# Another order of the 24 convolution units in the preparation of a gated delta rule: q before k in each head

## The chip, the core and the metric

The kernel runs on one core of one Trainium2 chip, written directly for its engines: TensorE (PE), VectorE (DVE), ScalarE (ACT), GpSimd (POOL) and the DMA queues, which run side by side and wait for each other on semaphores. The metric is the time of one execution on the device in microseconds; lower is better. All data is float32.

## The reference

The program is a network of two blocks on a sequence of 512 tokens of width 1024. The first block has differential attention, a gated delta rule in both directions and an expert-choice feed-forward layer of 16 experts; the second has a sparse attention mixer and a gated recurrence. The change lies in the preparation of q, k and v for the gated delta rule:

```python
h = rmsnorm(x, norm1_w[l])
p = jnp.einsum('bsd,dn->bsn', h, w_in[l])
...
qkv_g = jax.nn.silu(centred_depthwise_conv(qkv_g, conv_w[l]))   # 5 taps, each channel by itself
qg, kg, vg = jnp.split(qkv_g, [GDN_QK, 2 * GDN_QK], axis=-1)    # 8 heads of 128 each
qg = l2norm(qg.reshape(b, s, GDN_HEADS, GDN_DK))
kg = l2norm(kg.reshape(b, s, GDN_HEADS, GDN_DK))
vg = vg.reshape(b, s, GDN_HEADS, GDN_DV).astype(jnp.float32)
g_f = -jnp.exp(a_log_fwd[l]) * jax.nn.softplus(a_f + dt_bias_fwd[l])
...
o_fwd = gated_delta_rule_chunked(qg, kg, vg, g_f, beta_f)
```

## The kernel before

The kernel is a row of stages, each a block in which every engine has its own list of instructions; a stage ends when all its engines have ended. The stages are: norm and transposes, projections of the attention's q, k, v with rotation, attention (in whose gaps the first eight channel groups of the delta rule's input are already projected), the preparation that the change touches, the delta rule, output projections, the experts, and the second block.

In the preparation the 3072 channels are 24 units of 128 channels by 512 positions: unit h is q of head h (0 to 7), 8 + h is k, 16 + h is v. The eight q units lie ready in X (`raw_of`, units below `NEAR`). The k and v units have still to be projected by PE, each by eight matmuls (`project`, line 625), into one of four PSUM banks. The list `SEQ` gives the order in which units are worked on; before, it is k, q, v of head 0, then k, q, v of head 1, and so on. For one unit the work is:

- DVE: the convolution over five taps, one scaling (line 732) and four multiply-adds (line 735), into one of three buffers `conv[p % 3]`.
- ACT: silu in place (line 696). For q and k also the square (line 701) into one of two buffers `sq`.
- q and k: PE sums the square over the 128 channels with a matmul by ones (`sums`, line 634); ACT makes of it the reciprocal root by a logarithm and an exponential (`norm`, lines 199 and 200), behind a load of the function table (line 677; silu needs a load of its own, line 694); DVE multiplies (line 750), which ends the unit.
- k and v: PE turns the unit by four transposes (`turn`, line 649) and ACT copies the result out (`evac_turned`, line 685).

Every engine works strictly through its own list, and the lists are written out by hand. PE for head i: project v(i), sum k(i), project k(i+1), sum q(i), turn k(i), turn v(i). DVE: the convolutions in the order of `SEQ`, and behind the convolution at place p the multiplication of the unit at place p - 2. ACT: silu and square of k, silu and square of q, norm of k, silu of v, norm of q, the two evacuations. Beside this the gates of all heads are prepared once: small operations on DVE at its places 0 and 1, three small matmuls (lines 660 and 662) and three small exponentials (lines 710 to 712).

Of the kernel before, what the change touches and what calls it, by code (L numbers as in the profile page):

```python
# [14 lines left out]
ALU = mybir.AluOpType  # L15
ACT = mybir.ActivationFunctionType
# [7 lines left out]
HEADS = 8  # L24
# [87 lines left out]
def build(nc, io):  # L112
    ctx = ExitStack()
    counts = {}
    with ctx:
# [5 lines left out]
        def sem(name):  # L121

            return cleared.pop(0) if cleared else ctx.enter_context(nc.semaphore(name))
# [63 lines left out]
        def A():  # L187
            return Chain(nc.scalar, act_link, counts)
# [26 lines left out]
        def slab(slot, k=KD, cols=512):  # L215
            return SLB[slot][:, 0:k * cols].rearrange("p (k n) -> p k n", k=k)
# [198 lines left out]
        with nc.Block() as block:  # L415
# [177 lines left out]
        conv = [R[6][:, i * S:(i + 1) * S] for i in range(3)]  # L593
        sq = [R[6][:, 1536 + i * S:2048 + i * S] for i in range(2)]
        p3_done, conv_done, silu_done, sq3, ss3, rstd3, qk_norm, tr3, tr3_evac = [
            sem(n) for n in ("p3_done", "conv_done", "silu_done", "sq3", "ss3", "rstd3", "qk_norm", "tr3", "tr3_evac")]
        pre = {n: sem("p_" + n) for n in ("u_ready", "sp_ready", "g_ready", "cum_done", "G_ready", "pre_ready")}
        NC3 = 3 * HEADS

        SEQ = [u for i in range(HEADS) for u in (HEADS + i, i, 2 * HEADS + i)]  # L600
        POS = {u: p for p, u in enumerate(SEQ)}
        FAR = [u for u in SEQ if u >= NEAR]
        AT = {u: n for n, u in enumerate(FAR)}
        NORMED = [u for u in SEQ if u < 2 * HEADS]
        NTH = {u: n for n, u in enumerate(NORMED)}
# [8 lines left out]
        with nc.Block() as block:  # L614
            @block.tensor
            def _(pe):

                def project(n):
                    u = FAR[n]
                    i, j = (u - NEAR) // 4, u % 4  # L620
                    pe.wait_ge(slab_in[i], 48)
                    if n >= 4:
                        pe.wait_ge(conv_done, POS[FAR[n - 4]] + 1)
                    for k in range(KD):
                        m = pe.matmul(PS[n % 4][:, :], slab(i)[:, k, j * P:(j + 1) * P], hT[:, k, :],  # L625
                                      start=(k == 0), stop=(k == KD - 1))
                    m.then_inc(p3_done, 1)

                def sums(u):
                    n = NTH[u]  # L630
                    pe.wait_ge(sq3, n + 1)
                    if n >= 2:
                        pe.wait_ge(rstd3, n - 1)
                    pe.matmul(PS[4 + n % 2][:, :], ones, sq[n % 2], start=True, stop=True).then_inc(ss3, 1)

                def turn(u):
                    n = AT[u]
                    if u in NTH:
                        pe.wait_ge(qk_norm, NTH[u] + 1)
                        src = gk[:, u - HEADS, :]  # L640
                    else:
                        pe.wait_ge(silu_done, POS[u] + 1)
                        src = conv[POS[u] % 3]
                    if n >= 2:
                        pe.wait_ge(tr3_evac, n - 1)
                    else:
                        pe.wait_ge(pre["sp_ready"], 2)
                    for t in range(NT):
                        m = pe.transpose(PS[6 + n % 2][:, t * P:(t + 1) * P], src[:, t * P:(t + 1) * P], ident)
                    m.then_inc(tr3, 1)  # L650

                project(0)
                for i in range(HEADS):
                    k, q, v = SEQ[3 * i:3 * i + 3]
                    project(2 * i + 1)
                    sums(k)
                    if i == 0:
                        pe.wait_ge(pre["g_ready"], 1)
                        for d in range(2):
                            pe.matmul(v16(PS[6][:, 0:64])[:, :, 8 * d:8 * d + 8], (tri_le, tri_ge)[d],  # L660
                                      v16(gg)[:, :, 8 * d:8 * d + 8], start=True, stop=True)
                        pe.matmul(PS[7][:, 0:64], ones, gg, start=True, stop=True).then_inc(pre["cum_done"], 1)
                    if i + 1 < HEADS:
                        project(2 * i + 2)
                    sums(q)
                    turn(k)
                    turn(v)

            @block.scalar
            def _(act):  # L670
                a = A()
                cp = nc.scalar.activation

                def norm(u):

                    n = NTH[u]
                    nc.scalar.preload_act_table_set("natural_log_exp_and_others")
                    act.wait_ge(ss3, n + 1)
                    rsqrt(a, sq[n % 2], PS[4 + n % 2][:, :], 1.0, rstd3, LN_DK if u < HEADS else 0)

                def evac_turned(u):
                    n = AT[u]
                    act.wait_ge(tr3, n + 1)
                    dst = (gkt if u < 2 * HEADS else gv)[:, :, u % HEADS, :]
                    a(cp(dst, PS[6 + n % 2][:, :].rearrange("p (t d) -> p t d", t=NT), ACT.Copy), tr3_evac)

                act.wait_ge(pre["u_ready"], 1)
                a(cp(sb_, sb_, ACT.Exp, scale=-1.0))
                a(cp(sb_, sb_, ACT.Ln, bias=1.0))
                a(cp(al[:, 0:16], al[:, 0:16], ACT.Exp))  # L690
                a(cp(v16(beta), ab3[:, :, 16:32], ACT.Exp, scale=-1.0), pre["sp_ready"])
                for p, u in enumerate(SEQ):
                    if p % 3 != 1:
                        nc.scalar.preload_act_table(ACT.Silu)
                    act.wait_ge(conv_done, p + 1)
                    a(cp(conv[p % 3], conv[p % 3], ACT.Silu), silu_done)
                    if u in NTH:
                        n = NTH[u]
                        if n >= 2:
                            act.wait_ge(qk_norm, n - 1)  # L700
                        a(cp(sq[n % 2], conv[p % 3], ACT.Square), sq3)
                    if p % 3 == 1:
                        norm(SEQ[p - 1])
                    elif p % 3 == 2:
                        norm(SEQ[p - 1])
                        evac_turned(SEQ[p - 2])
                        evac_turned(u)
                    if p == 1:
                        act.wait_ge(pre["G_ready"], 1)
                        a(cp(eG, G, ACT.Exp))  # L710
                        a(cp(gl, PS[7][:, 0:64], ACT.Exp))
                        a(cp(decs, decs, ACT.Exp), pre["sp_ready"])

            @block.vector
            def _(dve):
                v = V()
                tt, stt = nc.vector.tensor_tensor, nc.vector.scalar_tensor_tensor
# [24 lines left out]
                for p in range(NC3 + 1):  # L742
                    if p < NC3:
                        convolve(p)
                    if 2 <= p and SEQ[p - 2] in NTH:
                        u = SEQ[p - 2]
                        n = NTH[u]
                        dve.wait_ge(rstd3, n + 1)
                        dst = gq[:, u, :] if u < HEADS else gk[:, u - HEADS, :]
                        v(tt(dst, conv[(p - 2) % 3], sq[n % 2], ALU.mult), qk_norm)  # L750
                    if p == 0:
                        for d in range(2):
                            v(nc.vector.tensor_scalar(cut[d], (tri_le, tri_ge)[d], BIG, -BIG, ALU.mult, ALU.add))
                        dve.wait_ge(pre["sp_ready"], 1)
                        v(stt(sa, sa, 0.0, sb_, ALU.max, ALU.add))
                        v(nc.vector.tensor_scalar(beta, beta, 1.0, None, ALU.add))
                        v(nc.vector.reciprocal(beta, beta))
                        v(stt(v16(gg), v16(sa), -1.0, al[:, 0:16].unsqueeze(1).to_broadcast([P, NT, 16]),
                              ALU.mult, ALU.mult), pre["g_ready"])
                    if p == 1:  # L760
                        dve.wait_ge(pre["cum_done"], 1)
                        v(nc.vector.tensor_copy(G, PS[6][:, 0:64]))
                        v(tt(decs, PS[7][:, 0:64], G, ALU.subtract), pre["G_ready"])
                    if p == 4:
                        dve.wait_ge(pre["sp_ready"], 2)
                        v(stt(nbeG, eG, -1.0, beta, ALU.mult, ALU.mult), pre["pre_ready"])
# [1475 lines left out]
```

## Time and profile before

| | us |
|---|---|
| median of 3 runs | 2635.56 |
| lowest and highest | 2632.33, 2638.42 |
| the profiled execution, its time | 2632.33 |
| its span | 2630.4 |
| PE busy | 2388.1 |
| DVE busy | 851.9 |
| ACT busy | 594.6 |
| POOL busy | 213.8 |

The profile is of one execution. The span runs from its first to its last instruction. Busy times add up what an engine's instructions lasted; the ends of matmuls are modelled. Each f32 matmul of 512 columns stands in the trace as two records. The granted clock is 1.00 at 2.4 GHz and 0.50 at 1.2 GHz. Over the whole program the mean was 0.979.

### The profile page before, as it was taken

The page shows a single profiled execution, that of the slowest core. Times are in us where ns is not written, and L with a number is a line of the kernel's source. Part 1 is how long each engine was busy: PE and PEld are TensorE (multiplying, and loading weights), DVE is VectorE, ACT ScalarE, POOL GpSimd, SP SyncE. Part 2 cuts the span into 40 slices and gives each one's busy share as a digit, 9 for nine tenths or more (in the row PEclk, how much of TensorE's full clock was granted, in tenths as well). Part 3 has the DMA queues.
Part 4 walks back from the last instruction along what each step waited for, and adds up shares of the span by engine and source line. Part 5 has one row for each costly group of instructions (what it writes and reads, how often), then busy time and mean ns, then how long its engine had stood idle before and what let it go on. Part 6 is the DMA issues. An engine that isn't in the chain of part 4 may idle for free. (4 is left out here: it accounts for less than half of the span.)

```text
span 2630.4 us, 26173 instructions
## 1 busy us (share of the span) xinstructions
PE 2388.1 (91%) x10644; PEld 1266.9 (48%) x10644; DVE 851.9 (32%) x1422; ACT 594.6 (23%) x1014; POOL 213.8 (8%) x166
## 2 busy tenths in 40 slices
PE   6999999899999998996998989888898976999878
PEld 3445554477887875444333333333333323575343
DVE  1215757633444442113010101101010104454672
ACT  2004647633333333101000000000000002223131
POOL 0000000133333430000000000000000000120000
PEclk9999999999999999997999999999999998999989
DMA  6101000010000004321999999999999991212001
GB/s 218 69 32 67 33 33 0 17 33 25 25 25 25 17 25 159 138 104 64 392 428 428 428 428 428 428 428 427 428 428 428 428 422 39 100 49 69 32 34 46
DMA packets 93386, 488.27 MB, mean 186 GB/s; under 512 B 10781, under 2 KB 37683, under 8 KB 68563
## 3 DMA queue, kind: packets, MB, share of 16 engines
q1 hardware_dynamic: 91920, 486.38, 45.5%
q8 instruction: 85, 1.39, 0.2%
q10 hardware_dynamic: 1347, 0.22, 0.0%
q14 instruction: 34, 0.28, 0.0%
HBM read 483.18 MB, written 3.41 MB: 185 GB/s over the span
## 5 line engine op out<-in xcount | busy, mean ns | idle before, releaser
L1365 PE MATMUL PS<-SL,R 128*64 128x512 f32 x1168 | 261.0, 595 | 39.4 <-DMA SL<-w_up 20.8
L1365 PE MATMUL PS<-R 128*64 128x512 f32 x880 | 197.3, 596 | 28.3 <-DMA R<-w_up 15.9
L1365 PEld LDWEIGHTS PS<-SL,R 128*64 128x64 f32 x1168 | 80.9, 137 | 214.7 <-issue 145.0
L1817 PE MATMUL PS<-HT,SL 128*128 128x512 f32 x384 | 169.2, 596 | 1.9 <-PEq L1560 1.9
L1006 ACT ACTIVATE SL<-PS 128x512 f32<-128x512 f32 x208 | 124.2, 597 | 122.0 <-PE PS L913 97.7
L1533 DVE TENSOR_TENSOR HT<-HT,PS 128x512 f32<-128x512 f32 x32 | 20.6, 684 | 369.9 <-PE PS L1365 369.9
L1385 PE MATMUL PS<-SL,HT 128*64 128x512 f32 x280 | 124.4, 594 | 14.8 <-ACT HT L1473 7.0
L1365 PEld LDWEIGHTS PS<-R 128*64 128x64 f32 x880 | 61.1, 137 | 159.1 <-issue 108.7
L1386 PE MATMUL PS<-SL,HT 128*64 128x512 f32 x280 | 124.9, 596 | 0.0
L343 PE MATMUL PS<-HT,SL 128*128 128x512 f32 x256 | 112.6, 593 | 3.5 <-PEq L230 2.6
L625 PE MATMUL PS<-HT,SL 128*128 128x512 f32 x256 | 114.9, 603 | 0.8 <-PEq L415 0.8
L1817 PEld LDWEIGHTS PS<-HT,SL 128*128 128x128 f32 x384 | 72.6, 191 | 89.2 <-issue 87.8
L1468 ACT ACTIVATE HT<-PS 128x512 f32<-128x512 f32 x32 | 17.4, 594 | 432.1 <-PE PS L1365 432.1
L1385 PE MATMUL PS<-R,HT 128*64 128x512 f32 x232 | 103.5, 594 | 12.2 <-ACT HT L1473 6.2
L887 PE MATMUL PS<-HT,X 128*128 128x512 f32 x256 | 112.9, 594 | 0.0
L1538 DVE COPY HT<-PS 64x512 f32<-64x512 f32 x16 | 10.9, 683 | 305.2 <-PE PS L1386 305.2
L1386 PE MATMUL PS<-R,HT 128*64 128x512 f32 x232 | 103.9, 596 | 0.0
L1684 POOL MEMSET R<- 64x512 f32 x1 | 0.5, 519 | 1198.4 <-POOLq L1560 1198.4
L1104 DVE TENSOR_TENSOR SL<-SL,PS 128x512 f32<-128x512 f32 x80 | 55.0, 688 | 132.4 <-PE PS L937 132.3
L1082 POOL TENSOR_TENSOR SL<-SL,tab 128x512 f32<-128x512 f32 x64 | 81.3, 1270 | 156.1 <-PE PS L924 153.5
L924 PE MATMUL PS<-SL 128*128 128x128 f32 x640 | 84.5, 275 | 0.0
L937 PE MATMUL PS<-SL 128*128 128x128 f32 x640 | 82.9, 281 | 0.1
(364 smaller groups left out, 3652.2 us busy)
## 6 DMA issues: line engine op xcount, KB each, us to landing
SL<-w_up SPq DMA_DIRECT2D x38, 2048.0 KB, 28.0
SL<-w_gate SPq DMA_DIRECT2D x35, 2048.0 KB, 30.1
SL<-w_down SPq DMA_DIRECT2D x35, 2048.0 KB, 27.3
R<-w_gate SPq DMA_DIRECT2D x29, 2048.0 KB, 30.1
R<-w_down SPq DMA_DIRECT2D x29, 2048.0 KB, 27.3
R<-w_up SPq DMA_DIRECT2D x26, 2048.0 KB, 28.7
SL<-w_in SPq DMA_DIRECT2D x19, 2048.0 KB, 9.0
X<-w_in SPq DMA_DIRECT2D x16, 512.0 KB, 3.9
```

Source lines behind the costliest of these rows:

```text
L343: m = pe.matmul(PS[u % 4][:, :], slab(g % 4)[:, k, j * P:(j + 1) * P], hT[:, k, :], start=(k == 0), stop=(k == KD - 1))
L625: m = pe.matmul(PS[n % 4][:, :], slab(i)[:, k, j * P:(j + 1) * P], hT[:, k, :], start=(k == 0), stop=(k == KD - 1))
L887: m_ = pe.matmul(extra_bank(i)[:, :], piece[m % 2][:, k, :], src[:, k, :], start=(k == 0), stop=(k == KD - 1))
L924: m = pe.matmul(part(bank(d, 0), i), B["A"][:, i, :], B["X"][:, i, :], start=True, stop=True)
L937: m = pe.matmul(part(bank(d, 1), i), W["XT"][:, i, :], B["PM"][:, i, :], start=True, stop=True)
L1006: a(nc.scalar.activation(flat(dst), src[:, :], ACT.Copy), done)
L1082: g(tt(B["A"], B["AT"], all4((up, low)[d][l]), ALU.mult), E4["BT_ready"])
L1104: v(tt(B["X"], B["X"], f4(bank(d, 1)[:, :]), ALU.subtract), E4["X_ready"])
L1365: m = pe.matmul(banks[n][half * CAP:(half + 1) * CAP, :], XC[x // 2 % 2][:, 2 * j + k, toks], w[:, k, (2 * half + n) * 512:(2 * half + n + ...
L1385: pe.matmul(DB[0:CAP, :], hk, w[:, k, 0:512], start=first, stop=last)
L1386: m = pe.matmul(DB[CAP:P, :], hk, w[:, k, 512:1024], start=first, stop=last)
L1817: m = pe.matmul(bank_[:, :], slab(i % 2)[:, k, j * P:(j + 1) * P], hT[:, k, :], start=(k == 0), stop=(k == KD - 1))
```

## The change

The units of a head come in the order q, k, v. With it the hand-written lists of the three engines are rewritten: PE sums the square of the unit at place p - 1, and the turns of a head come behind the sum of the next head's q; ACT does the norm of the unit at place p - 1 ahead of silu at place p, and loads the table for silu at every place; DVE multiplies one convolution behind instead of two. The small work on the gates is at place 2 instead of 1. What is computed is the same.

```diff
--- before.py
+++ after.py
@@ -597,7 +597,7 @@
         pre = {n: sem("p_" + n) for n in ("u_ready", "sp_ready", "g_ready", "cum_done", "G_ready", "pre_ready")}
         NC3 = 3 * HEADS
 
-        SEQ = [u for i in range(HEADS) for u in (HEADS + i, i, 2 * HEADS + i)]
+        SEQ = [u for i in range(HEADS) for u in (i, HEADS + i, 2 * HEADS + i)]
         POS = {u: p for p, u in enumerate(SEQ)}
         FAR = [u for u in SEQ if u >= NEAR]
         AT = {u: n for n, u in enumerate(FAR)}
@@ -649,22 +649,22 @@
                         m = pe.transpose(PS[6 + n % 2][:, t * P:(t + 1) * P], src[:, t * P:(t + 1) * P], ident)
                     m.then_inc(tr3, 1)
 
-                project(0)
-                for i in range(HEADS):
-                    k, q, v = SEQ[3 * i:3 * i + 3]
-                    project(2 * i + 1)
-                    sums(k)
-                    if i == 0:
+                for p in range(NC3 + 2):
+                    if 1 <= p <= NC3 and SEQ[p - 1] in NTH:
+                        sums(SEQ[p - 1])
+                    if p == 2:
                         pe.wait_ge(pre["g_ready"], 1)
                         for d in range(2):
                             pe.matmul(v16(PS[6][:, 0:64])[:, :, 8 * d:8 * d + 8], (tri_le, tri_ge)[d],
                                       v16(gg)[:, :, 8 * d:8 * d + 8], start=True, stop=True)
                         pe.matmul(PS[7][:, 0:64], ones, gg, start=True, stop=True).then_inc(pre["cum_done"], 1)
-                    if i + 1 < HEADS:
-                        project(2 * i + 2)
-                    sums(q)
-                    turn(k)
-                    turn(v)
+                    if p >= 4 and p % 3 == 1:
+                        turn(SEQ[p - 3])
+                        turn(SEQ[p - 2])
+                    if p < NC3 and p % 3 == 1:
+                        project(AT[SEQ[p + 1]])
+                    elif p == 0 or p + 2 < NC3 and p % 3 == 2:
+                        project(AT[SEQ[p + 2 if p else 1]])
 
             @block.scalar
             def _(act):
@@ -689,27 +689,26 @@
                 a(cp(sb_, sb_, ACT.Ln, bias=1.0))
                 a(cp(al[:, 0:16], al[:, 0:16], ACT.Exp))
                 a(cp(v16(beta), ab3[:, :, 16:32], ACT.Exp, scale=-1.0), pre["sp_ready"])
-                for p, u in enumerate(SEQ):
-                    if p % 3 != 1:
+                for p in range(NC3 + 3):
+                    if 1 <= p <= NC3 and SEQ[p - 1] in NTH:
+                        norm(SEQ[p - 1])
+                    if p < NC3:
                         nc.scalar.preload_act_table(ACT.Silu)
-                    act.wait_ge(conv_done, p + 1)
-                    a(cp(conv[p % 3], conv[p % 3], ACT.Silu), silu_done)
-                    if u in NTH:
-                        n = NTH[u]
-                        if n >= 2:
-                            act.wait_ge(qk_norm, n - 1)
-                        a(cp(sq[n % 2], conv[p % 3], ACT.Square), sq3)
-                    if p % 3 == 1:
-                        norm(SEQ[p - 1])
-                    elif p % 3 == 2:
-                        norm(SEQ[p - 1])
-                        evac_turned(SEQ[p - 2])
-                        evac_turned(u)
-                    if p == 1:
+                        act.wait_ge(conv_done, p + 1)
+                        a(cp(conv[p % 3], conv[p % 3], ACT.Silu), silu_done)
+                        if SEQ[p] in NTH:
+                            n = NTH[SEQ[p]]
+                            if n >= 2:
+                                act.wait_ge(qk_norm, n - 1)
+                            a(cp(sq[n % 2], conv[p % 3], ACT.Square), sq3)
+                    if p == 2:
                         act.wait_ge(pre["G_ready"], 1)
                         a(cp(eG, G, ACT.Exp))
                         a(cp(gl, PS[7][:, 0:64], ACT.Exp))
                         a(cp(decs, decs, ACT.Exp), pre["sp_ready"])
+                    if p >= 5 and p % 3 == 2:
+                        evac_turned(SEQ[p - 4])
+                        evac_turned(SEQ[p - 3])
 
             @block.vector
             def _(dve):
@@ -742,12 +741,12 @@
                 for p in range(NC3 + 1):
                     if p < NC3:
                         convolve(p)
-                    if 2 <= p and SEQ[p - 2] in NTH:
-                        u = SEQ[p - 2]
+                    if 1 <= p and SEQ[p - 1] in NTH:
+                        u = SEQ[p - 1]
                         n = NTH[u]
                         dve.wait_ge(rstd3, n + 1)
                         dst = gq[:, u, :] if u < HEADS else gk[:, u - HEADS, :]
-                        v(tt(dst, conv[(p - 2) % 3], sq[n % 2], ALU.mult), qk_norm)
+                        v(tt(dst, conv[(p - 1) % 3], sq[n % 2], ALU.mult), qk_norm)
                     if p == 0:
                         for d in range(2):
                             v(nc.vector.tensor_scalar(cut[d], (tri_le, tri_ge)[d], BIG, -BIG, ALU.mult, ALU.add))
@@ -757,7 +756,7 @@
                         v(nc.vector.reciprocal(beta, beta))
                         v(stt(v16(gg), v16(sa), -1.0, al[:, 0:16].unsqueeze(1).to_broadcast([P, NT, 16]),
                               ALU.mult, ALU.mult), pre["g_ready"])
-                    if p == 1:
+                    if p == 2:
                         dve.wait_ge(pre["cum_done"], 1)
                         v(nc.vector.tensor_copy(G, PS[6][:, 0:64]))
                         v(tt(decs, PS[7][:, 0:64], G, ALU.subtract), pre["G_ready"])
```

PE, head 1 to the start of head 2, before. PS0 to PS3 are the banks of the projections (PS3 takes v of head 1, PS0 takes k of head 2, PS1 takes v of head 2), PS4 and PS5 those of the sums, PS6 and PS7 those of the turns; R6 holds the squares.

```order
L625 MATMUL PS3<-HT,SL2 128x512 x8
L634 MATMUL PS4<-R6,tab 128x512
L625 MATMUL PS0<-HT,SL0 128x512 x8
L634 MATMUL PS5<-R6,tab 128x512
L649 MATMUL PS6<-tab,R12 128x128 x4
L649 MATMUL PS7<-tab,R6 128x128 x4
L625 MATMUL PS1<-HT,SL2 128x512 x8
```

The same place of the changed kernel:

```order
L625 MATMUL PS3<-HT,SL2 128x512 x8
L634 MATMUL PS5<-R6,tab 128x512
L625 MATMUL PS0<-HT,SL0 128x512 x8
L634 MATMUL PS4<-R6,tab 128x512
L649 MATMUL PS6<-tab,R12 128x128 x4
L649 MATMUL PS7<-tab,R6 128x128 x4
L625 MATMUL PS1<-HT,SL2 128x512 x8
```

The kinds stand as before, and the two sums have changed banks: the second one, ahead of the turns, is that of q of head 1 before, and that of q of head 2 now.

DVE, from the convolution of v of head 1 (read from PS3) on, before. A convolution's first operation is line 732; X holds the q units; the operation into R12 is the multiplication that ends a unit.

```order
L732 TENSOR_SCALAR R6<-PS3,small 128x512
L735 SCALAR_TENSOR_TENSOR R6<-PS3,small,R6 128x510
L735 SCALAR_TENSOR_TENSOR R6<-PS3,small,R6 128x511 x2
L735 SCALAR_TENSOR_TENSOR R6<-PS3,small,R6 128x510
L750 TENSOR_TENSOR R12<-R6 128x512
L732 TENSOR_SCALAR R6<-PS0,small 128x512
```

The same place of the changed kernel, where the scaling is line 731, the multiply-add 734 and the multiplication 749:

```order
L731 TENSOR_SCALAR R6<-PS3,small 128x512
L734 SCALAR_TENSOR_TENSOR R6<-PS3,small,R6 128x510
L734 SCALAR_TENSOR_TENSOR R6<-PS3,small,R6 128x511 x2
L734 SCALAR_TENSOR_TENSOR R6<-PS3,small,R6 128x510
L749 TENSOR_TENSOR R12<-R6 128x512
L731 TENSOR_SCALAR R6<-X,small 128x512
```

Behind v's convolution and k's multiplication stood the convolution of the next k; now the next q's stands there, and the next k's behind that.

ACT, one head before, from silu of k to the evacuations:

```order
L694 ACT_TABLE_LOAD
L696 ACTIVATE R<-R 128x512
L701 ACTIVATE R<-R 128x512
L696 ACTIVATE R<-R 128x512
L701 ACTIVATE R<-R 128x512
L677 ACT_TABLE_LOAD
L199 ACTIVATE R<-PS,small 128x512
L200 ACTIVATE R<-R 128x512
L694 ACT_TABLE_LOAD
L696 ACTIVATE R<-R 128x512
L677 ACT_TABLE_LOAD
L199 ACTIVATE R<-PS,small 128x512
```

The changed kernel from silu of q on, where silu is line 698, its table load 696 and the square 703:

```order
L696 ACT_TABLE_LOAD
L698 ACTIVATE R<-R 128x512
L703 ACTIVATE R<-R 128x512
L677 ACT_TABLE_LOAD
L199 ACTIVATE R<-PS,small 128x512
L200 ACTIVATE R<-R,small 128x512
L696 ACT_TABLE_LOAD
L698 ACTIVATE R<-R 128x512
L703 ACTIVATE R<-R 128x512
L677 ACT_TABLE_LOAD
L199 ACTIVATE R<-PS,small 128x512
L200 ACTIVATE R<-R 128x512
```

A table load now stands between the square of the first unit and silu of the second, and a head has five loads instead of four. The exponentials of the gates have got a load of their own.

## Rows read from the trace of the kernel before

**Rows 1.** The page, busy us, share of the span, instructions: PE.

```profile
PE 2388.1 (91%) x10644; PEld 1266.9 (48%) x10644; DVE 851.9 (32%) x1422; ACT 594.6 (23%) x1014; POOL 213.8 (8%) x166
```

**Rows 2.** Windows: stretch, length, busy us by engine, granted clock, DMA share, GB/s.

```profile
434.00:451.00 17.00, 17.00 (x47) 7.92 (x46) 13.01 (x19) 12.85 (x17) 0.00 (x0) 1.00 0.00 0
```

**Rows 3.** Timeline of one head: start, us, engine, line, operation, count, [idle before <-releaser].

```profile
434.30 7.03 PE L625 MATMUL PS<-HT,SL 128*128 128x512 f32 x16
...
441.16 1.02 PE L634 MATMUL PS<-R,tab 128*128 128x512 f32 x2
441.42 0.75 DVE L732 TENSOR_SCALAR R<-PS,small 128x512 f32<-128x512 f32 x1 [3.11 <-PE PS L625]
442.02 1.04 PE L649 MATMUL PS<-tab,R 128*128 128x128 f32 x8
...
442.89 7.03 PE L625 MATMUL PS<-HT,SL 128*128 128x512 f32 x16
442.94 0.72 ACT L200 ACTIVATE R<-R,small 128x512 f32<-128x512 f32 x1
...
444.94 1.28 ACT L694 ACT_TABLE_LOAD   x1
445.35 0.69 DVE L750 TENSOR_TENSOR R<-R 128x512 f32<-128x512 f32 x1
446.14 0.49 DVE L732 TENSOR_SCALAR R<-X,small 128x512 f32<-128x512 f32 x1
446.24 0.63 ACT L696 ACTIVATE R<-R 128x512 f32<-128x512 f32 x1
...
449.87 0.63 ACT L696 ACTIVATE R<-R 128x512 f32<-128x512 f32 x1 [2.34 <-DVE R L735]
...
450.53 0.63 ACT L701 ACTIVATE R<-R 128x512 f32<-128x512 f32 x1
```

**Rows 4.** Timeline of the stage's start.

```profile
367.49 16.39 PE L625 MATMUL PS<-HT,SL 128*128 128x512 f32 x32 [0.84 <-PEq L415]
...
377.12 0.75 DVE L732 TENSOR_SCALAR R<-PS,small 128x512 f32<-128x512 f32 x1 [8.92 <-PE PS L625]
...
383.72 1.02 PE L634 MATMUL PS<-R,tab 128*128 128x512 f32 x2
...
385.19 7.08 PE L625 MATMUL PS<-HT,SL 128*128 128x512 f32 x16
...
386.58 0.23 DVE L762 COPY small<-PS 128x64 f32<-128x64 f32 x1
...
387.10 0.75 DVE L732 TENSOR_SCALAR R<-PS,small 128x512 f32<-128x512 f32 x1
```

**Rows 5.** Timeline of the stage's end.

```profile
498.74 1.02 PE L634 MATMUL PS<-R,tab 128*128 128x512 f32 x2
...
500.19 1.12 PE L634 MATMUL PS<-R,tab 128*128 128x512 f32 x2 [0.43 <-ACT R L701]
...
502.93 0.69 DVE L750 TENSOR_TENSOR R<-R 128x512 f32<-128x512 f32 x1
503.67 0.66 PE L649 MATMUL PS<-tab,R 128*128 128x128 f32 x4 [2.36 <-DVE R L750]
...
504.81 0.66 PE L649 MATMUL PS<-tab,R 128*128 128x128 f32 x4 [0.48 <-ACT R L696]
...
507.54 1.23 ACT L685 ACTIVATE R<-PS 128x512 f32<-128x512 f32 x2
```

**Rows 6.** Windows behind a wait at the stage's end, at the next stage's start, around 2429.

```profile
505.00:506.00 1.00, 0.46 (x4) 0.22 (x3) 0.00 (x0) 1.00 (x1) 0.00 (x0) 0.74 0.00 0
511.00:512.00 1.00, 0.95 (x4) 0.95 (x5) 0.00 (x0) 0.00 (x0) 0.00 (x0) 0.50 1.07 326
...
2426.00:2430.00 4.00, 1.91 (x7) 0.90 (x6) 3.75 (x9) 3.53 (x5) 0.00 (x0) 1.00 0.01 3
```

**Rows 7.** Timeline of PE at 2429.

```profile
2429.15 0.91 PE L1711 MATMUL PS<-R 128*128 128x384 f32 x2 [2.09 <-ACT R L1924]
```

## The prediction

> **What bounds the stage now.** I read four views: the busy totals and the granted clock of each stage, then the windows of the stage that the change touches (367.5 to 508.8 us), then one head of it in order of time on all engines, then its start and its end. Over the span PE is busy 2388.1 of 2630.4 us [rows 1], and inside the stage it is busy 17.00 of 17 us at full clock, with DVE at 13.01 and ACT at 12.85 [rows 2]. So PE sets the pace here, and the one thing to ask is whether PE still finds its inputs ready.
>
> One head in PE's order [rows 3]: a projection takes 441.16 - 434.30 = 6.86 us, a sum over a square 442.02 - 441.16 = 0.86, the two turns together 442.89 - 442.02 = 0.87. Two projections, two sums and the turns are 16.31 us a head, without a gap. DVE waits on PE instead: its convolution at 441.42 had been waiting 3.11 us [rows 3]. What stands after this stage (the gated delta rule, the experts) starts behind it, so I count what it gains or loses one for one.
>
> **What the change does to PE.** Away from the two ends PE's order of kinds does not change: project v(i), sum k(i), project k(i+1), a sum, turn k(i), turn v(i). What changes is whose square that second sum reads: q(i) before, q(i+1) after. Before, q(i) was convolved long ahead: a q's silu is at 449.87 and its square at 450.53, and its sum starts near 457.5, one period of 16.3 after the q sum at 441.16 [rows 3]. After, q(i+1) is convolved behind v(i) and behind the multiplication that ends k(i), since DVE works in order, and v(i) cannot be convolved before its projection is done.
>
> The chain from the end of project v(i), which is the start of sum k(i), to the sum over q(i+1), all from starts in [rows 3]:
> - PE to DVE, 441.42 - 441.16 = 0.26
> - convolution of v(i) from PSUM with the hop, 445.35 - 441.42 = 3.93
> - multiplication that ends k(i), 446.14 - 445.35 = 0.79
> - convolution of q(i+1) from X with the hop to ACT, 449.87 - 446.14 = 3.73
> - silu, 450.53 - 449.87 = 0.66
> - square 0.63 and about 0.05 to PE, 0.68
>
> Together 10.05 us. PE has sum k(i) and project k(i+1) to do meanwhile, 0.86 + 6.86 = 7.72. It waits 10.05 - 7.72 = 2.33 us. A sum issued after a wait also cannot load its weights in the shadow of the matmul before: the one such sum in the stage lasts 1.12 against 1.02 for the usual [rows 5], so I add 0.10. That is 2.43 us a head, and the period becomes 18.74.
>
> Nothing catches this up. Behind the waiting sum on PE's queue stand both turns and project v(i+1), and the next chain starts only at the end of that projection. The other inputs are early: k(i)'s norm needs its sum's ScalarE part, ready 443.66 - 441.16 = 2.50 us after the sum starts, while the multiplication comes 4.19 after it [rows 3]. The convolution of k(i+1) starts behind that of q(i+1), near 8.7, and ends near 12.6; silu and square of it end near 15.2, before 18.74. So sum k never waits.
>
> **How often.** The sums over q1 to q7 wait, seven of them; q0 is in X from the start and is convolved while project k0 runs (DVE stood idle for 8.92 us before 377.12, [rows 4]). At q1, DVE has the two small operations on the cumulated gates between, 387.10 - 386.58 = 0.52 us more, and PE has the three small matmuls, 385.19 - 383.72 - 0.86 = 0.61 us of cover more [rows 4]. So the first wait is 2.33 + 0.52 - 0.61 + 0.10 = 2.34 us, and the sum is 2.34 + 6 x 2.43 = **16.9 us**.
>
> **The ends.** q0's sum now stands between project k0 and project v0, so one sum more (0.86) lies ahead of project v7's end. DVE's multiplication that ends k stays behind the convolution of v, so only q's moves, and nothing waits for q's before the next stage. In exchange the end is shorter. Before, from sum k7 at 498.74 to the end of the last evacuation at 507.54 + 1.23 = 508.77 is 10.03 us, because ACT still had to load a table and do q7's norm behind silu v7 [rows 5]. After, q7 is done: turn k7 starts (503.67 - 502.93) = 0.74 after its multiplication begins, at 0.26 + 3.93 + 0.74 = 4.93; turn v7 0.43 later, ending near 6.0 (a turn there lasts 0.66); then the second evacuation of 0.62, so near 7.0. That is **-3.05**. If ACT or a cold clock spoils it, 0; that end is kept for the range.
>
> **ACT.** The order shows nine table loads more: one for each head, because before, silu of k and of q shared a load and now each of the three silus of a head has its own, and one for the exponentials of the gates. One load lasts 1.28 and the next ACTIVATE starts 446.24 - 444.94 = 1.30 after it [rows 3]: 9 x 1.30 = 11.7 us. I cost them at nothing. After silu v(i) (over at 4.9 after sum k(i) starts) ACT evacuates for 1.23 (the pair's row, [rows 5]) and loads until about 7.4, and silu q(i+1) has its input only at 8.71: cover of 1.3 us. At the gates it is tight: wait for them at 5.5, load 1.30, three small ones 0.8, load 1.30 gives about 9.0 against 9.2. If that cover were gone the price is a few tenths, once.
>
> The page ScalarE: Activation LUTs of the Trainium skill (section What ACT_TABLE_LOAD costs) gives about 2.66 us for each switch, load and drain together. By that rule ACT would reach norm k(i+1) and then silu q late, and I work out some 2 us more a head, 12 in all, a time near 2662. The rows of this stage, with the next ACTIVATE 1.30 behind the start of the load, speak against it [rows 3].
>
> **Sum.** 16.9 + 0.86 - 3.05 = **+14.7 us**. Against the profiled execution, 2632.33 us (span 2630.4 and 1.9 around it), that is 2647.0. This execution was the lowest of the three; against their median of 2635.56 it is 2650.3. I forecast **2650**.
>
> **The rivals.**
> *The clock falls in the waits.* After waits with little around them PE was put to 1.2 GHz: in this stage's end, 2.36 us of wait and short turns, the clock was 0.74 in 505 to 506 [rows 5, 6]. At the half level project k0 took 377.12 - 0.26 - 367.49 = 9.37 instead of 6.86 [rows 4], 2.5 us. If each of seven waits brought that, 17.5 us more: 2668. Against it: a wait of 2.09 us between wide matmuls left the clock at 1.00 [rows 6, 7], and mine is 2.33 with a dense 7 us on either side. Between these two it can happen at some of them. 14 in 100.
>
> *The wait isn't there.* PE's work is the same in amount, only ordered otherwise; if the chain is covered after all (DVE's convolutions overlapping more than their starts show), the sum is 0.86 - 3.05 = -2.2, or 2633. The page Perfetto Trace Analysis of the Trainium skill (section Identifying Performance Opportunities) says that performance generally improves by improving the most-contended engine; read alone, it would give this case, as PE's busy time isn't touched. DVE works in order, and the steps of the chain are taken from start to start, so what overlap there is, is already in them. 5 in 100.
>
> *Not slower, even faster.* Place: the end of the stage. Before, the clock had fallen by 506 and the next stage began at the low level [rows 6]. If the shorter end kept it up, the next matmuls save up to 2.5 us, which with -2.2 gives 2631. It decides only if the seven waits together are under about 4.7 us, that is a chain of 8.4 us or less instead of 10.05. 3 in 100.
>
> *ACT binds.* By the table loads, 2662: 2 in 100.
>
> My forecast, with waits of 1.8 to 3 us and the clock up or down once or twice: 76 in 100, its own range 2645 to 2657. The range for 8 in 10 takes in part of the clock rival: **2643 to 2664**. This kernel's runs can tell 0.2%, 5.3 us, from no change. Faster needs more than either favourable case gives: 0.02. Same: the two cases of no wait and a small wait, 0.07. Slower: 0.91.
>
> **What would show it.** In the profile after: PE idle before the sums of line 634 seven times, about 2.2 to 2.5 us each, released by ACT's square; sums of k without idle; period near 18.7; granted clock still 1.00 in the stage; the stage (first projection to the last evacuation) near 156 us instead of 141.3; DVE waiting longer for each projection of v; ACT with 41 or so table loads of 1.28 us instead of 32 and its busy share in the stage hardly lower; PE's busy total unchanged. Wrong if PE's idle before these sums is under 1 us, if it is released by a table load or by norm instead, or if the clock drops to 0.5 behind the waits.

## The result and the profile after

| | before | after |
|---|---|---|
| median, us | 2635.56 (5 runs) | 2661.61 (5 runs) |
| lowest and highest | 2632.33, 2640.03 | 2659.29, 2663.67 |
| profiled execution, its span | 2632.33, 2630.4 | 2661.32, 2659.4 |

The ratio is 1.0097, with a 95% interval of 1.0084 to 1.0111: slower by 26 us, between 22 and 29. The forecast was 2650, 14.7 us slower, with a range that ends at 2664; the measured median is 2.4 us inside that end.

The busy totals of the changed kernel, the row that answers to [rows 1]:

```profile
span 2659.4 us, 26174 instructions
...
PE 2405.9 (90%) x10644; PEld 1277.6 (48%) x10644; DVE 851.5 (32%) x1422; ACT 606.1 (23%) x1023; POOL 213.9 (8%) x166
```

The counts tell that PE does the same matmuls, and still its busy time is 17.8 us more, 9.0 of them in the stage: some matmuls ran slower. ACT has its nine loads more, 11.5 us.

Who waited for whom on PE from the stage's start to the next stage's first matmuls, in the changed kernel (engine, line, releaser: us in total, times, longest):

```profile
PE PS L634 <- ACT R L703: 14.1, 7, 2.0
PE PS L649 <- ACT R L685: 4.6, 1, 4.6
PE PS L862 <- POOL X L1056: 3.0, 1, 3.0
```

The first row is the wait that the prediction spoke of: seven sums, released by the square. Before, no such wait stood in the heads. One head in order of time, changed kernel, for [rows 3]:

```profile
444.32 1.02 PE L634 MATMUL PS<-R,tab 128*128 128x512 f32 x2
444.58 0.75 DVE L731 TENSOR_SCALAR R<-PS,small 128x512 f32<-128x512 f32 x1 [5.46 <-PE PS L625]
...
448.51 0.69 DVE L749 TENSOR_TENSOR R<-R 128x512 f32<-128x512 f32 x1
...
449.23 0.49 DVE L731 TENSOR_SCALAR R<-X,small 128x512 f32<-128x512 f32 x1
...
450.41 1.28 ACT L696 ACT_TABLE_LOAD   x1
452.89 0.63 ACT L698 ACTIVATE R<-R 128x512 f32<-128x512 f32 x1 [1.20 <-DVE R L734]
...
453.55 0.63 ACT L703 ACTIVATE R<-R 128x512 f32<-128x512 f32 x1
...
454.24 1.12 PE L634 MATMUL PS<-R,tab 128*128 128x512 f32 x2 [2.03 <-ACT R L703]
455.20 1.04 PE L649 MATMUL PS<-tab,R 128*128 128x128 f32 x8
```

The chain from sum k(i) to sum q(i+1) is 454.24 - 444.32 = 9.92 us, each link within 0.07 of the forecast (10.05). The added load ends at 451.69 and ACT then still waits 1.20 us for DVE, so the load is off the path. The period is 18.62 us instead of 16.31.

But not in every head. Windows of the changed kernel, two periods from sum k to sum k, and a stretch behind the second one's wait (length, busy us of PE, PEld, DVE, ACT, POOL, granted clock, DMA, GB/s), for [rows 2, 6]:

```profile
444.32:462.94 18.62, 16.59 (x45) 7.58 (x44) 12.36 (x17) 13.48 (x16) 0.00 (x0) 1.00 0.00 0
462.94:483.24 20.30, 18.27 (x45) 8.65 (x44) 12.37 (x17) 13.48 (x16) 0.00 (x0) 0.92 0.00 1
473.20:476.50 3.30, 3.30 (x11) 2.19 (x10) 2.32 (x4) 2.58 (x4) 0.00 (x0) 0.50 0.00 0
```

Same work, same wait, and the second period lasts 1.68 us longer, because behind its wait the granted clock was at the lower of its two levels, 1.2 GHz, for about 3.4 us. I call such a stretch a fall. This happened behind four of the seven waits, near 398, 473, 493 and 514 us. The sum behind such a wait shows it, 1.88 instead of 1.12 us:

```profile
463.80 7.03 PE L625 MATMUL PS<-HT,SL 128*128 128x512 f32 x16
472.86 1.88 PE L634 MATMUL PS<-R,tab 128*128 128x512 f32 x2 [2.03 <-ACT R L703]
474.53 1.91 PE L649 MATMUL PS<-tab,R 128*128 128x128 f32 x8
```

The end of the stage, changed kernel, for [rows 5]:

```profile
523.84 1.02 PE L634 MATMUL PS<-R,tab 128*128 128x512 f32 x2
...
528.02 0.63 ACT L698 ACTIVATE R<-R 128x512 f32<-128x512 f32 x1 [0.47 <-DVE R L734]
528.02 0.69 DVE L749 TENSOR_TENSOR R<-R 128x512 f32<-128x512 f32 x1
528.68 1.23 ACT L685 ACTIVATE R<-PS 128x512 f32<-128x512 f32 x2
...
529.43 1.94 PE L649 MATMUL PS<-tab,R 128*128 128x128 f32 x8 [4.56 <-ACT R L685]
...
531.47 0.60 ACT L685 ACTIVATE R<-PS 128x512 f32<-128x512 f32 x1 [0.26 <-PE PS L649]
```

From sum k7 to the end of the last evacuation it is 532.07 - 523.84 = 8.23 us, against 10.03 before: 1.80 shorter, not 3.05. Turn k7 (the two turns are one row, at 529.43) was not released by DVE's multiplication but by ACT's evacuation of head 6, at 529.43 instead of the 528.77 forecast.

**Where the time is.** I take the stage from its first projection to the first matmul of the next one. Before it is 511.05 - 367.49 = 143.56 us, after 534.35 - 369.08 = 165.27: 21.7 more. That adds up: one sum more ahead and the start 0.9, the waits 2.08 + 6 x 2.30 = 15.9, four low stretches 6.7, the end -1.8. The spans differ by 29.0: 1.6 lie ahead of the stage, where the programs do the same, and 5.7 behind it, where they also do the same. Of these I speak last.

### The profile page after: what moved, and what is told of

Its sections match the earlier page's. It is cut to its first block and busy times, and to the rows that moved or that the text cites. A ratio compares the mean times of both kernels' runs of the same rounds, so it can differ in the third digit from the quotient of the medians.

```text
span 2659.4 us, 26174 instructions
## 1 busy us (share of the span) xinstructions
PE 2405.9 (90%) x10644; PEld 1277.6 (48%) x10644; DVE 851.5 (32%) x1422; ACT 606.1 (23%) x1023; POOL 213.9 (8%) x166
```

## The experiments

All figures in one table first. Stage is the length as above, from the profile of each kernel; falls are the stretches at 1.2 GHz behind the seven waits; ratio is to the runs of before on the same chip. "Beside before" is the median less that of before on the same chip.

| kernel | wait at a sum, us | falls | stage, us | median, beside before, us | ratio, interval |
|---|---|---|---|---|---|
| before | none | 0 | 143.56 | | |
| after | 2.03 | 4 | 165.27 | +26.1 | 1.0097, 1.0084 to 1.0111 |
| e1, waits filled | 0.31 | 0 | 157.42 | +13.4 | 1.0056, 1.0043 to 1.0069 |
| e2, k's multiplication late | 1.31 | 0 | 153.64 | +9.4 | 1.0036, 1.0024 to 1.0049 |
| e3, six loads fewer | 2.09 | 7 | 169.75 | +26.1 | 1.0105, 1.0091 to 1.0119 |
| e4, before with eight loads more | none | 0 | 142.94 | +0.3 | 1.0000, 0.9991 to 1.0009 |
| e5, q one head ahead | none | 0 | 141.67 | -3.4 | 0.9990, 0.9981 to 0.9999 |
| e6, evacuation early | 2.03 | 6 | 168.39 | +28.4 | 1.0099, 1.0083 to 1.0114 |
| e7, after again | 2.03 | 4 | 165.13 | (one run, 2659.21) | |
| e8, before again | none | 0 | 143.96 | (one run, 2634.21) | |
| e9, 25 matmuls ahead | none | 0 | 165.47 | +23.1 | 1.0086, 1.0072 to 1.0100 |
| e10, 16 matmuls ahead | none | 0 | 157.80 | +12.3 | 1.0048, 1.0034 to 1.0062 |
| e11, 8 matmuls ahead | none | 0 | 150.66 | +8.1 | 1.0028, 1.0018 to 1.0038 |

### e1: the waits filled with matmuls

The changed kernel with this, called ahead of each of the seven sums (the calls and two semaphore waits are left out here); the fillers' results are overwritten.

```diff
+                def fill(n):
+                    ...
+                    for k in range(2):
+                        pe.matmul(PS[n % 4][:, :], slab(i)[:, k, j * P:(j + 1) * P], hT[:, k, :],
+                                  start=True, stop=True)
```

> The changed kernel with two more matmuls of 128x512 columns on PE right ahead of each of the seven sums over q1 to q7; their results are overwritten by the next projection. In the changed kernel's profile these sums wait 1.89 to 2.03 us, and behind four of the seven the clock is 0.50 for a while; the four periods with it are 1.7 us longer. Theory A (the chain over v's convolution makes the wait, and the wait makes the clock fall): the fillers, 0.86 us each, lie inside the wait, PE's idle time there falls to about 0.3 us, the period stays 18.6 us, the clock stays 1.00, and 4 x 1.7 = 6.7 us are gained: 2655, stage 156.3 us instead of 163.0. Rival B (the clock falls by itself or by the mean load of the whole stage, not by the single wait): falls stay, 2661. Rival C (PE's queue is the limit, not the chain): the period grows by 2 x 0.86 us, 12 us more: 2674.

One head of it, PE alone; line 659 is the filler:

```profile
438.28 1.02 PE L634 MATMUL PS<-R,tab 128*128 128x512 f32 x2
439.14 7.03 PE L625 MATMUL PS<-HT,SL 128*128 128x512 f32 x16
446.01 1.88 PE L659 MATMUL PS<-HT,SL 128*128 128x512 f32 x4
448.20 1.12 PE L634 MATMUL PS<-R,tab 128*128 128x512 f32 x2 [0.32 <-ACT R L715]
```

And the window over all heads of the same kernel:

```profile
375.00:512.00 137.00, 134.95 (x358) 61.82 (x357) 91.12 (x128) 100.45 (x120) 0.00 (x0) 1.00 0.00 0
```

The chain is the same 448.20 - 438.28 = 9.92 us, so PE's queue is not what limits (rival C fell). Over all heads the clock is 1.00, and the stage is 7.85 us shorter though PE does fourteen matmuls more (0.8 of it because the low stretch at the stage's start was shorter in this trace: project k0 took 8.60 us and not 9.44; 0.3 at the end; the four falls, 6.7, are the rest). So the clock does not fall by itself, and the falls go when the waits are filled: theory A fits. Of rival B one half stays open. The fillers shorten each wait and raise PE's busy share over the whole stage at once, and so does e2, so neither tells a single wait from the mean load. For the single wait speaks that each fall in the traces began with the sum or the turns right behind a wait. Beside before, the median came down from +26.1 to +13.4 us, 4.9 more than the stage did.

### e2: the multiplication of k behind the next q's convolution

```diff
-                    if 1 <= p and SEQ[p - 1] in NTH:
-                        u = SEQ[p - 1]
+                    at = p - 1 if p % 3 == 1 else p - 2
+                    if p >= 1 and p % 3 != 2:
+                        u = SEQ[at]
...
-                        v(tt(dst, conv[(p - 1) % 3], sq[n % 2], ALU.mult), qk_norm)
+                        v(tt(dst, conv[at % 3], sq[n % 2], ALU.mult), qk_norm)
```

> The changed kernel with one part of its DVE list undone: the multiplication that ends k(i) stands behind the convolution of q(i+1) instead of ahead of it. Theory A: the chain from the end of project v(i) to the sum of q(i+1) is shorter by the multiplication, 0.69 + 0.03 = 0.72 us, so each wait falls from 2.03 to 1.3 us, the period from 18.62 to 17.9: 7 x 0.72 = 5.0 us. With waits of 1.3 us the clock should not fall either, 6.7 us more: 2650, stage 151.3 us. If the clock still falls four times: 2656.6. Rival D (ACT, with its table loads, makes the wait, so DVE's order doesn't matter): 2661, waits still 2.0.

PE's waits in it, one period from sum k to sum k, and the window over the heads:

```profile
PE PS L634 <- ACT R L703: 9.0, 7, 1.3
```

```profile
457.20 1.02 PE L634 MATMUL PS<-R,tab 128*128 128x512 f32 x2
...
466.40 1.12 PE L634 MATMUL PS<-R,tab 128*128 128x512 f32 x2 [1.31 <-ACT R L703]
...
475.10 1.02 PE L634 MATMUL PS<-R,tab 128*128 128x512 f32 x2
```

```profile
380.00:510.00 130.00, 120.99 (x325) 55.58 (x324) 89.44 (x125) 98.92 (x118) 0.00 (x0) 1.00 0.00 0
```

The wait is 0.72 shorter and the period 475.10 - 457.20 = 17.90, exactly what the multiplication on the chain costs, and no wait of 1.31 us brought a fall (clock 1.00 over all heads). The stage was expected 151.3 + 2.3 (in the length used here) = 153.6 and is 153.64. DVE's order makes the wait; ACT does not (rival D fell). One kind of instruction moved in one list gave back 16.7 of the 26 us.

### e3 and e4: the table loads alone

e3 leaves the load ahead of q's silu out of the changed kernel for heads 2 to 7, e4 puts one into the kernel before for all eight heads:

```diff
-                        nc.scalar.preload_act_table(ACT.Silu)
+                        if p < 4 or p % 3:
+                            nc.scalar.preload_act_table(ACT.Silu)
```

```diff
-                    if p % 3 != 1:
-                        nc.scalar.preload_act_table(ACT.Silu)
+                    nc.scalar.preload_act_table(ACT.Silu)
```

> The changed kernel without the load of silu's table ahead of q of heads 2 to 7 and without the one ahead of q of head 1 kept (that one is kept): six loads of 1.28 us fewer on ACT, since silu's table is still there from v. Theory A: ACT waited 1.2 us for the convolution behind that load anyway, so nothing changes: 2661, waits 2.03, within 2 us. Rival D (the added loads are on the path): six times up to 1.3 us less, 2653 or, with fewer clock falls, 2650.

> The kernel before with the one part of the change that adds work: a load of silu's table ahead of q's silu too, eight loads of 1.28 us more on ACT. Theory A: hidden, because a q's sum comes 6.3 us behind its square: 2635.6, within 2 us, stage 141.3 us. Rival D: up to 8 x 1.3 = 10 us more, 2646.

The waits of e3, PE and ACT, over the stage, and last ACT's row of the changed kernel:

```profile
PE PS L634 <- ACT R L704: 14.4, 7, 2.1
...
ACT R L699 <- DVE R L735: 21.0, 17, 2.6
```

```profile
ACT R L698 <- DVE R L734: 12.9, 17, 1.3
```

e3's waits are not shorter, its median is the same, +26.1. What ACT no longer loads, 6 x 1.28 = 7.7 us, it waits for DVE: 21.0 us instead of 12.9. In e4 ACT is busy 14.13 of 17 us, which is [rows 2]'s 12.85 and one load of 1.28:

```profile
434.00:451.00 17.00, 17.00 (x47) 7.86 (x46) 13.00 (x19) 14.13 (x18) 0.00 (x0) 1.00 0.00 0
```

PE stays at 17.00, and the ratio is 1.0000. So the loads, the only work that the change adds, cost nothing that can be measured, as forecast. The Trainium skill (ScalarE: Activation LUTs, What ACT_TABLE_LOAD costs) puts a switch to another set at about 2.66 us, 1.28 for the load and 1.38 for a drain. The load agrees, the drain is not seen here: at a real switch, from the norm's functions to silu, the next ACTIVATE starts 446.24 - 444.94 = 1.30 us after the load's start [rows 3].

### e5: q one head ahead, but in front of v

The kernel before with another `SEQ`, q0's sum ahead of project v0, and the ends of the lists fitted to it:

```diff
-        SEQ = [u for i in range(HEADS) for u in (HEADS + i, i, 2 * HEADS + i)]
+        SEQ = [0] + [u for i in range(HEADS) for u in (HEADS + i, i + 1, 2 * HEADS + i) if u != HEADS or i == 0]
```

> The kernel before with q one head ahead: the order q0, then k0 q1 v0, k1 q2 v1 and so on to k6 q7 v6, k7 v7. PE's list is that of the changed kernel (sum k(i), project k(i+1), sum q(i+1), turns of i, project v(i+1)), but DVE convolves q(i+1) ahead of v(i) instead of behind it. Theory A: the sum of q(i+1) is ready, PE doesn't wait anywhere in the heads, period 16.3 us; one sum more at the start (0.86) and the end shorter by up to 3.05: 2633.4, no difference from before that can be measured, stage near 139 us. Rival E (summing q of the next head, or the sums' banks and squares in that order, is what costs): it keeps the waits, near 2660.

PE's waits in it, both at the stage's end, the window over all heads, and the end itself:

```profile
PE PS L649 <- DVE R L762: 3.9, 1, 3.9
PE PS L875 <- POOL X L1069: 3.2, 1, 3.2
```

```profile
375.00:497.00 122.00, 122.00 (x331) 57.38 (x330) 91.33 (x128) 91.41 (x114) 0.00 (x0) 1.00 0.00 0
```

```profile
497.04 1.02 PE L634 MATMUL PS<-R,tab 128*128 128x512 f32 x2
501.97 1.09 PE L649 MATMUL PS<-tab,R 128*128 128x128 f32 x8 [3.91 <-DVE R L762]
...
506.24 2.08 PE L875 MATMUL PS<-tab,small 128*128 128x128 f32 x8 [3.17 <-POOL X L1069]
```

PE sums the next head's q here too, as in the changed kernel, and is busy 122.00 of 122 us. So it isn't PE's order and not the earlier q as such: it is that DVE took q behind v. And this version has the shorter end in full: turn k7 starts 501.97 - 497.04 = 4.93 us after sum k7, released by the multiplication, and from sum k7 to the next stage's first matmul it is 506.24 - 497.04 = 9.20 us instead of before's 511.05 - 498.74 = 12.31. That is 3.11 shorter, where the forecast for the changed kernel was 3.05. It is the fastest of all versions, 2631.90 against before's 2635.30, but the ratio of 0.9990 is only a hair outside no difference.

### e6: the evacuations ahead of silu v

The changed kernel; ACT evacuates the turned units of each head ahead of the next k's norm and the next v's silu.

```diff
+                    if 5 <= p < NC3 and p % 3 == 2:
+                        evac_turned(SEQ[p - 4])
+                        evac_turned(SEQ[p - 3])
                     if 1 <= p <= NC3 and SEQ[p - 1] in NTH:
                         norm(SEQ[p - 1])
...
-                    if p >= 5 and p % 3 == 2:
+                    if p == NC3 + 2:
                         evac_turned(SEQ[p - 4])
                         evac_turned(SEQ[p - 3])
```

> The changed kernel with ACT's two evacuations of the turned units of head i moved ahead of the norm of k(i+1) and silu of v(i+1). It asks for the missing part of the shorter end: in the changed kernel the turn of k7 started 5.6 us after sum k7 and not 4.9, released by the evacuation of head 6. Theory F (turn k7 waited for its PSUM bank, held by turn k6 until ACT had done silu v7): turn k7 starts 4.9 us after sum k7, released by DVE's multiplication, the end is 0.7 to 1.2 us shorter, the rest unchanged: 2660.5, waits 2.03. Rival: the low clock alone made the end longer; no change in the start of turn k7.

```profile
526.55 1.02 PE L634 MATMUL PS<-R,tab 128*128 128x512 f32 x2
...
530.74 0.69 DVE L752 TENSOR_TENSOR R<-R 128x512 f32<-128x512 f32 x1
...
531.48 1.97 PE L649 MATMUL PS<-tab,R 128*128 128x128 f32 x8 [3.91 <-DVE R L752]
```

Turn k7 now starts 4.93 us after sum k7, the very figure of the prediction, and is released by the multiplication. Theory F holds: it had waited for its PSUM bank. From sum k7 to the next stage it is 536.43 - 526.55 = 9.88 us instead of 10.51, 0.63 shorter, a little less than the 0.7 to 1.2 expected: the two turns still last 1.97 us, at the low clock, against 1.09 in e5 at its end. The stage as a whole is 3.1 us longer, since in this trace six waits brought a fall instead of four. The median did not reach the 2660.5 expected either: 2663.73, and the ratio can't be told from after's.

### e7 and e8: both kernels again

> The changed kernel once more, unchanged, for a second trace. The question is whether the four clock falls of seven stand at fixed places. If the fall depends on where a wait lies against something that runs by itself, their number changes (3 to 6) or their places do, with the period 18.62 between falls the same; the stage is 163 us plus or minus 1.7 for each fall more or less. Outside the stage the same kernel before shows low-clock stretches at other places too, which would differ by a few us from trace to trace.

> The kernel before once more, unchanged, for a second trace. Stage 141.3 us within 0.3, no clock fall between 375 and 500 us; low-clock stretches elsewhere (behind 1215, 2184, 2362, 2464, 2515 us) may differ by 1.7 us each, which would tell how much of the difference outside the stage is no effect of the change.

In e7 the waits are 2.03 again (1.89 the first), the falls again four, but near 396, 416, 491 and 512 us: behind the first, second, sixth and seventh wait, not the first, fifth, sixth and seventh. e3 had seven, e6 six, each with waits of about 2.0. The program is the same in both traces; so which wait brings a fall is not set by the program. Before showed no fall in its heads, twice.

### e9 to e11: a pure delay

The kernel before with 25, 16 or 8 matmuls more ahead of the first projection:

```diff
+                pe.wait_ge(slab_in[0], 48)
+                for _ in range(25):
+                    pe.matmul(PS[0][:, :], slab(0)[:, 0, 0:P], hT[:, 0, :], start=True, stop=True)
```

> The kernel before with 25 more matmuls of 128x512 columns at the start of the stage, ahead of the first projection, into the bank that this overwrites. It asks for the part of the changed kernel's 26 us that its stage (21.7 us longer) does not hold. Each lasts 0.86 us at full clock, 25 of them 21.4 us, with no wait and no clock fall in the heads; since the stage starts at the low clock, its slow stretch of about 2.5 us falls on the fillers and not on project k0, with the same cost. Theory G (the rest of the difference is scatter of low-clock stretches from trace to trace): 2635.3 + 21.4 = 2656.7. Rival H (whatever ends the stage later makes the part behind it slower too, by about 4 us, since the low-clock stretches there lie at other places then): 2661.

> The same with 16 matmuls, 13.7 us, the size of the shift that the changed kernel with fillers in its waits had. Theory G: 2649.0. Rival H: about 2653, if it does not depend on the size of the shift; if it goes by where the shift puts the later stretches, anything from 2649 to 2653.

> The same with 8 matmuls, 6.9 us, near the shift that the changed kernel with the late multiplication had (10 us). Theory G: 2642.2. Rival H: 2642 to 2646, and other than for 25 and 16 matmuls.

Measured beside before: +23.1, +12.3, +8.1 us, against stages longer by 21.9, 14.2 and 7.1. The differences are +1.2, -1.9 and +1.0, on both sides of zero, and each within what its interval leaves (2.6 to 3.7 us to either side). Theory G fits all three. Of rival H, 4 us more whatever the delay is outside the intervals of e10 (14.2 + 4 against at most 16.3) and e11 (7.1 + 4 against at most 10.0). For 25 matmuls alone it isn't excluded: 21.9 + 4 = 25.9 lies inside the interval of e9, 19.0 to 26.4. For what is left open see the next section.

## Why the prediction was right, and where it was short

- **PE's inputs come late, in seven sums**: right, in place, releaser and number. e2 and e5 show the cause: the wait follows DVE's chain to the hundredth, and is gone when q stands ahead of v. The rival without a wait fell with it.
- **The size of a wait**: the row shows 2.03 idle; from start to start it is 9.92 - 7.72 = 2.20, since the row's matmuls reach 0.17 past the next start, and with 0.10 for the sum behind it the period grew by 2.30 where I had 2.43. The first wait cost 2.08 instead of 2.34, all seven 15.9 instead of 16.9. Two links, the multiplication and q's convolution, were 0.07 shorter each.
- **The load of a sum's weights behind a wait**: 1.12 against 1.02, right: the load starts together with the sum, at 454.24:

```profile
454.24 0.30 PEld L634 LDWEIGHTS PS<-R,tab 128*128 128x128 f32 x2 [2.85 <-ACT R L703]
```

- **The table loads cost nothing**: right, shown from both sides by e3 and e4.
- **The end**: -1.80 instead of -3.05. The step that failed: I let turn k7 wait for DVE's multiplication alone. It also needs the bank that turn k6 holds until ACT has evacuated it, and ACT does that behind silu v7. It is 0.66 us late, and the turns then ran at the low clock. e6 shows the first part, and e5, which has neither, has the end as forecast.
- **The clock**: this is the term that was mis-sized. I gave it as a rival, at 14 in 100, for a fall behind each wait, and counted it with nothing in the sum. It fell behind four of seven in both traces, 1.68 us each, 6.7 in all. My own signs of being wrong named it (the clock at 0.5 behind the waits), and it came; so did more busy time of PE, 17.8 us, where I had none. My two rows were a wait of 2.09 us without a fall and one of 2.36 with, and I took 2.3 for safe because dense work stands around it. With waits of about 2 us (1.89 to 2.09) it comes in 21 of 28 (four traces), at 1.31 in none of seven, at 0.31 in none of seven. So on a PE that is otherwise full a wait of 2 us can already bring it; between 1.31 and 1.89 nothing was measured. The price per fall was also off: 2.5 us, taken from a stretch at the stage's start, where it was 1.7.
- **What isn't explained.** The stage holds 21.7 us, the medians differ by 26, interval 22 to 29. In the traces of before the part behind the stage lasts 2119.35 and 2121.55 us, of after 2125.05 and 2124.65, with the same instructions. Much of it is low clock at other places. The first matmuls of the experts last 9.08 us before and 10.41 after:

```profile
1239.88 9.08 PE L1347 MATMUL PS<-R 128*128 128x128 f32 x64 [1.11 <-DVE R L1526]
1262.54 10.41 PE L1346 MATMUL PS<-R 128*128 128x128 f32 x64 [1.11 <-DVE R L1525]
```

  The kernel e4 has before's stage and before's median, and its trace shows 10.55 there and 2125.5 us behind the stage; e9, the pure delay, 2125.4; e10 and e11, 2121.6 and 2122.5. So the long form comes without the change too. But it does not look like pure scatter: in the five traces whose stage ends latest, behind 532 us (after, e7, e3, e6 and the pure delay e9), the part behind it lasts 2124.65 to 2126.07 us, in the other eight 2119.35 to 2125.5. That speaks for a form of rival H, that a late end of the stage by itself makes the rest slower, though e9's trace is of its slowest run, 2661.74 us where its median is 2658.85. More falls inside the stage in unprofiled runs (e3 had seven, its stage 4.5 us longer) explain the 4 us badly, since the profiled run with four falls took 2661.32 us, close to the median. I leave the 4 us open.

The forecast of 14.7 would have been 15.0 with the start, the waits and the end as measured, and 21.7 with the falls. In the first sum two errors of 1.0 and 1.25 us nearly cancel, the waits too dear and the end too short. The measured 2661.6 lies outside the 2645 to 2657 of my forecast proper; the wider range held because it reached into the clock rival, and about 4 us of what it had to hold are unexplained. That it held is in part luck.

## What to carry to other kernels

Where one engine is full and each engine works through a list in order, an order is judged by one sum: from the end of the bound engine's last output, through all that stands ahead in the other engines' lists, to the input that it needs next, against the work it has meanwhile. Put what has its inputs early (q, ready in X) ahead of what waits for the bound engine (v), not behind it. And give the fall of TensorE's clock a price already for waits of 2 us amid dense work: here three in four of them brought one, and each added 1.7 us.

## What the runs showed of the hardware

- A PE that works 16.6 of 18.6 us and then waits 2.03 us can be put from 2.4 to 1.2 GHz for about 3.4 us. Behind which wait it happens changes between two executions of one program.
- Fourteen matmuls whose results nobody reads, put into the waits, made the stage about 7 us shorter: the granted clock was 1.00 over all heads, and no fall came.
- A load of ScalarE's function table lasts 1.28 us also where the same table is already there: eight such loads in e4 added 14.13 - 12.85 = 1.28 us a head to its busy time, and none to the kernel's.
